# Output projections of two mixers as products of rounded halves, and modulation chunks moved, in a TensorE-bound float32 model on one core

## The reference

```python
def first_block(x, c, ...):
    for l in range(DEPTH):                      # DEPTH = 2; m = 3 l, 3 l + 1, 3 l + 2
        mod = (silu(c) @ ada_w[l] + ada_b[l]).reshape(b_, N_SUB, 3, D_MODEL)
        y = swiglu(modulate(x, mod[:, 0, 0], mod[:, 0, 1]), ffn_w13[l, 0], ffn_w2[l, 0])
        x = layer_norm(ALPHA * x + 0.5 * (1 + mod[:, 0, 2]) * y, ln_g[l, 0], ln_b[l, 0])
        y = token_mixer(modulate(x, mod[:, 1, 0], mod[:, 1, 1]), w_in[l], w_out[l], ...)
        x = layer_norm(ALPHA * x + (1 + mod[:, 1, 2]) * y, ln_g[l, 1], ln_b[l, 1])
        y = swiglu(modulate(x, mod[:, 2, 0], mod[:, 2, 1]), ffn_w13[l, 1], ffn_w2[l, 1])
        x = layer_norm(ALPHA * x + 0.5 * (1 + mod[:, 2, 2]) * y, ln_g[l, 2], ln_b[l, 2])

def token_mixer(h, w_in, w_out, ...):
    qkv_a, a_a, b_a, z_a, qkv_b, qk_c, v_c, i_c, f_c, o_c = jnp.split(h @ w_in, IN_SPLITS, axis=-1)
    ...   # oa: gated delta rule (384 wide), ob: attention (256), hc: mLSTM (384), each with its norm
    return jnp.concatenate([oa, ob, hc], axis=-1) @ w_out
```

## Time and profile before

| | before |
|---|---|
| median of 3 runs | 1808.94 us (1808.0 to 1812.43) |
| profiled execution | 1810.99 us, span 1809.2 us |
| mean granted TensorE clock | 0.986 of full speed |
| TensorE busy | 1714.5 us (95%), 12816 matmul records |
| VectorE busy | 1286.6 us (71%), 1938 instructions |
| ScalarE busy | 743.7 us (41%), 971 instructions |
| loads of ring chunks | 302 of 1024 KB, 5.6 us from issue to landing (median), and 2 of the condition |
| HBM read | 326.77 MB, 181 GB/s over the span |

### The profile page before, as it was taken

One profiled execution on the slowest core, in us unless ns is written; L12 is line 12 of the kernel. 1 busy time (PEld: TensorE's weight loads), 2 busy tenths in 40 slices (PEclk: granted clock), 3 DMA queues, 4 the chain that ended last, 5 costly groups with the idle time before them and its releaser, 6 DMA issues. The chain is left out here.

```text
span 1809.2 us, 30057 instructions
## 1 busy us (share of the span) xinstructions
PE 1714.5 (95%) x12816; PEld 1496.0 (83%) x12816; DVE 1286.6 (71%) x1938; ACT 743.7 (41%) x971; POOL 6.3 (0%) x14
## 2 busy tenths in 40 slices
PE   2999989999999999998899999999989999999998
PEld 2999979877999989998888789998834556747898
DVE  7876787856877786677976568897794778326744
ACT  2433375333533453335642264343322445224354
POOL 0000000000000000000000000000000000000000
PEclk9999999999999999999999999999989999999999
DMA  9877535443577737662546147774373010321102
GB/s 390 347 279 280 195 117 222 166 161 117 233 279 293 289 141 279 248 264 94 205 155 240 68 169 278 281 277 183 149 280 129 1 47 1 126 95 47 47 24 93
DMA packets 48516, 329.77 MB, mean 182 GB/s; under 512 B 5224, under 2 KB 8448, under 8 KB 9344
## 3 DMA queue, kind: packets, MB, share of 16 engines
q1 hardware_dynamic: 47520, 324.69, 46.7%
q0 software_dynamic: 864, 3.17, 0.6%
HBM read 326.77 MB, written 1.07 MB: 181 GB/s over the span
## 5 line engine op out<-in xcount | busy, mean ns | idle before, releaser
L332 PE MATMUL ps<-xhi,low 128*128 128x256 f32 x2048 | 501.1, 284 | 4.2 <-ACT xhi L1390 4.2
L332 PEld LDWEIGHTS ps<-xhi,low 128*128 128x128 f32 x2048 | 362.4, 192 | 5.9 <-ACT xhi L1390 5.2
L332 PE MATMUL ps<-xhi,whi_wk 128*128 128x256 f32 x1072 | 297.8, 287 | 39.8 <-ACT xhi L1390 38.9
L1390 ACT ACTIVATE wk<-ps 128x256 f32<-128x256 f32 (+5 forms) x219 | 108.6, 504 | 490.5 <-PE ps L332 425.0
L332 PE MATMUL ps<-xa,ring 128*128 128x256 f32 (+1 forms) x1056 | 287.0, 430 | 10.0 <-issue 4.8
L332 PE MATMUL ps<-xlo,whi_wk 128*128 128x256 f32 x1072 | 290.6, 280 | 0.0
L332 PEld LDWEIGHTS ps<-xa,ring 128*128 128x128 f32 x1056 | 200.4, 192 | 91.1 <-issue 62.0
L1390 ACT ACTIVATE whi_wk<-ring 128x2048 fp32r<-128x2048 f32 x100 | 191.5, 1918 | 159.2 <-DMA ring<-in_stream_dram 95.3
L332 PEld LDWEIGHTS ps<-xhi,whi_wk 128*128 128x128 f32 x1072 | 202.6, 194 | 42.8 <-issue 41.1
L1967 DVE TENSOR_TENSOR low<-ring,whi_wk 128x2048 fp32r<-128x2048 f32 (+1 forms) x101 | 228.4, 2264 | 6.6 <-ACT whi_wk L1390 6.6
L332 PE MATMUL ps<-wk 64*64 64x64 f32 (+10 forms) x2712 | 210.3, 262 | 5.8 <-ACT wk L1390 4.3
(11 more groups left out here) (131 smaller groups left out, 2547.9 us busy)
## 6 DMA issues: line engine op xcount, KB each, us to landing
ring<-in_stream_dram SPq DMA_DIRECT2D x302, 1024.0 KB, 5.6
ring<-in_cond_dram SPq DMA_DIRECT2D x2, 1024.0 KB, 4.8
wk<-spread_dram POOLq DMA_DIRECT2D x4, 384.0 KB, 5.2
wk<-spread_dram POOLq DMA_DIRECT2D x2, 768.0 KB, 7.5
tab<-in_tab_dram SPq DMA_DIRECT2D x1, 1440.0 KB, 20.4
res<-in_xt_dram SPq DMA_DIRECT2D x1, 1024.0 KB, 17.5
res<-in_ct_dram SPq DMA_DIRECT2D x1, 1024.0 KB, 9.2
out_dram<-wk SPq DMA_DIRECT2D x4, 256.0 KB, 2.4
```

The costliest lines, as they stand in the source:

```text
L332: last[0] = nc.tensor.matmul(o, l, r, start=start, stop=stop, skip_group_check=free)
L1390: return nc.scalar.activation(o, i, f, **kw)
```

## The change

- **Halves in the output projections** (m = 1 and 4). Each w_out chunk takes two places (`take_both`), so the four fill all eight. ScalarE rounds the four chunks (`out_weights_high`) and the eight result tiles (`result_high`, into `ohi`), VectorE makes both low parts (`out_weights_low`, `result_low`, into `whi_xa`), and each of the 64 products becomes three (`terms`). In TensorE's order "lx2" now stands ahead of `early(1, ...)`.
- **The mixer's start**: the `l2` sums move behind projection 5 and "p6.0"; ScalarE and VectorE copy projection 5 ahead of them (`gate_or_copy(9)`). The first chunk's halves are made in the FFN before (tile 20), and ScalarE's `normed` moves from the norm into the mixer, behind `win_high(m, 4)`. The rows r_u, r_ab and r_ln get other storage. `win_low(6)` goes ahead of `rows()`, and the wait for projections 3 to 5 moves to a later point on TensorE.
- **The norm behind a mixer**: the low parts of the next FFN's first two weight chunks move from the norm's start to behind the folded squares and behind the tokens' low parts.
- **Modulation chunks of m = 7**: six (FFN_MODS) go into FFN m = 3, two stay in MLA's front, which thus holds 6 instead of 16 chunks, and four (LAST_MODS) go into MLA's output projection. The condition is loaded four times instead of twice.

```diff
+        ohi = nc.alloc_sbuf_tensor_at("ohi", [P, KT, T], F32R, offset=wk_at + 4 * (SCR + 8960))
...
-        LATE_MODS = [(6, ch) for ch in range(GATE, 12)] + [(7, ch) for ch in range(12)]
-        LATE_AT = (0, 2, 4, 7, 10, 13, 16)
+        FFN_MODS = [(7, ch) for ch in range(6)]
+        LATE_MODS = [(6, ch) for ch in range(GATE, 12)] + [(7, 6), (7, 7)]
+        LATE_AT = (0, 1, 2, 3, 4, 5, 6)
+        LAST_MODS = [(7, ch) for ch in range(GATE, 12)]
+        COND_AFTER = (("var", 2), ("var", 4), ("var", 5), ("pt", MLA_H - 1))
...
+            return 0 if (m, ch) in FFN_MODS else 2 if (m, ch) in LATE_MODS else 3 if (m, ch) in LAST_MODS else 1
...
+                    if m == 3 and 2 <= p < 8:
+                        leave("ada", *FFN_MODS[p - 2])
...
-                    if i == 4:
-                        for p in range(3):
-                            eng.wait_ge(*step_of("proj_read", m, p))
-                        eng.wait_ge(scalar_done, step("l2sq", m))
-                        for t in range(6):
-                            mm(banks(1, 1536)[:, 256 * t:256 * t + 256], blk, tiles(g_sq, 256)[:, t], True, True)
-                        last[0].then_inc(tensor_done, 1)
-                        done.named("l2", m)
-                fill(2)
+                fill(1)
...
+                for p in range(3):
+                    eng.wait_ge(*step_of("proj_read", m, p))
+                eng.wait_ge(scalar_done, step("l2sq", m))
+                for t in range(6):
+                    mm(banks(1, 1536)[:, 256 * t:256 * t + 256], blk, tiles(g_sq, 256)[:, t], True, True)
+                last[0].then_inc(tensor_done, 1)
+                done.named("l2", m)
+                fill(1)
...
                 eng.wait_ge(vector_done, step("rows", m))
-                for p in range(3, 6):
-                    eng.wait_ge(*step_of("proj_read", m, p))
...
                 eng.wait_ge(scalar_done, step("ekd", m))
+                for p in range(3, 6):
+                    eng.wait_ge(*step_of("proj_read", m, p))
...
-                        w_out[ch] = tiles(take("wout", l, ch), 256)
-                        w_held[ch] = held[0]
-                    for k in range(5):
-                        mm(bank(ch, 256 * t, 256 * t + 256), w_out[ch][:, k, P * t:P * t + P], xa[:, k, CS], k == 0 and t == 0, False, free=True)
+                        no = w_held[ch] = take_both("wout", l, ch)
+                        w_out[ch] = tiles(low[:, (no + 1) % RING, :], 256), tiles(low[:, no % RING, :], 256)
+                        eng.wait_ge(vector_done, step("owlow", m, ch))
+                    terms(ch, t, (3, 4, 0, 1, 2))
+                def terms(ch, t, ks):
+                    (hi, lo), at_t, o = w_out[ch], slice(P * t, P * t + P), bank(ch, 256 * t, 256 * t + 256)
+                    for k in ks:
+                        if ch in (0, 1):
+                            eng.wait_ge(vector_done, step("ol", m, k))
+                        mm(o, hi[:, k, at_t], ohi[:, k, :], k == 3 and t == 0, False, free=True)
+                        mm(o, lo[:, k, at_t], ohi[:, k, :], False, False, free=True)
+                        mm(o, hi[:, k, at_t], whi_xa[:, k, XS], False, k == KT - 1, free=True)
                 eng.wait_ge(vector_done, step("oa_done", m))
                 eng.wait_ge(scalar_done, step("mo", m, 1))
+                fill(1)
                 early(1, 0)
                 early(1, 1)
...
-                fill(1)
...
-                        for k in range(5, 8):
-                            mm(bank(ch, 256 * t, 256 * t + 256), w_out[ch][:, k, P * t:P * t + P], xa[:, k, CS], False, k == KT - 1, free=True)
+                        terms(ch, t, (5, 6, 7))
...
+                leave("cond2", 3)
+                for c in range(4):
+                    leave("ada", *LAST_MODS[c])
...
+            def out_weights_high(m, ch):
+                n = found["chunk_no", "wout", m // 3, ch][1]
+                eng.wait_ge(landed[n % RING], loads(n))
+                eng.wait_ge(*step_of("chunk", n + 1 - RING))
+                act(low[:, (n + 1) % RING, :], ring[:, n % RING, :], ACT.Copy, "owround", m, ch).then_inc(scalar_done, 1)
...
+                if to_ffn:
+                    normed(m)
+            def normed(m):
...
+                    if kind == "w13" and j == 20 and f == 0:
+                        win_high(m + 1, 0)
+                    if m in (3, 5) and kind == "w13" and j == 2:
+                        conditions(m // 5)
...
                 win_high(m, 4)
+                normed(m - 1)
...
+                eng.wait_ge(tensor_done, step("proj", m, 5))
+                gate_or_copy(9, bank(6, 256, 512), "proj_read_a", m, 5)
                 one_table()
                 eng.wait_ge(tensor_done, step("l2", m))
                 log_mean(g_tt, banks(1, 1536), 1, EPS, "l2e", m)
                 root(g_tt, "ri", m)
...
                 fill(11)
+                out_weights_high(m, 1)
...
+                eng.wait_ge(tensor_done, step("oa", m))
+                for k in (3, 4):
+                    result_high(k)
+                eng.wait_ge(vector_done, step("oa_done", m))
+                for k in range(3):
+                    result_high(k)
+                for ch in (2, 3):
+                    out_weights_high(m, ch)
                 eng.wait_ge(vector_done, step("lcen", m))
                 act(l_sq, l_h, ACT.Square, "lsq", m).then_inc(scalar_done, 1)
+                out_weights_high(m, 0)
                 eng.wait_ge(tensor_done, step("lvar", m))
...
-                eng.wait_ge(vector_done, step("oa_done", m))
+                for k in range(5, 8):
+                    eng.wait_ge(vector_done, step("mix", m, k))
+                    result_high(k)
...
-                if to_ffn:
+                if to_ffn and m % 3 != 1:
                     lows(m + 1, 0)
-                elif m < 5:
-                    win_low(m + 1, 0)
+                elif m % 3 == 0:
                     win_low(m + 1, 1)
...
                 if m == 5:
                     context(0)
+                if m % 3 == 1:
+                    lows(m + 1, 0)
...
+                    else:
+                        lows(m + 1, 1)
...
+                        if m == 3 and 2 <= j // 2 < 8:
+                            mod_part(*FFN_MODS[j // 2 - 2])
...
+                def out_weights_low(ch):
+                    n = found["chunk_no", "wout", l, ch][1]
+                    eng.wait_ge(scalar_done, step("owround", m, ch))
+                    tt(low[:, n % RING, :], ring[:, n % RING, :], low[:, (n + 1) % RING, :].bitcast(F32), SUB, "owlow", m, ch).then_inc(vector_done, 1)
+                def result_low(k):
+                    eng.wait_ge(scalar_done, step("oh", m, k))
+                    tt(whi_xa[:, k, XS], xa[:, k, CS], ohi[:, k, :].bitcast(F32), SUB, "ol", m, k).then_inc(vector_done, 1)
+                out_weights_low(1)
                 fill(len(BESIDE) - at["n"])
+                for k in (3, 4, 0, 1, 2):
+                    result_low(k)
+                out_weights_low(2)
                 eng.wait_ge(tensor_done, step("lmu", m))
                 eng.wait_ge(vector_done, done.count)
                 stt(l_h, banks(6, 768), -1.0 / HD, l_h, MUL, ADD, "lcen", m).then_inc(vector_done, 1)
+                for ch in (3, 0):
+                    out_weights_low(ch)
                 eng.wait_ge(scalar_done, step("mixed_a", m))
...
+                for k in range(5, 8):
+                    result_low(k)
+                found["mixed", m] = found["ol", m, 7]
...
-                for c in range(6):
+                for c in range(2):
...
-                for c in range(6, 10):
+                for c in range(2, 4):
...
-                for c in range(10, 16):
+                for c in range(4, 6):
...
+                    if ch:
+                        mod_part(*LAST_MODS[ch - 1])
+                mod_part(*LAST_MODS[3])
```

More of the change, by code:

```diff
@@ L226, in build @@
         g_t, g_tt, g_dt, g_at, g_att = [W(SCR + 1536 * i, 1536) for i in range(5)]
-        r_u, r_ab, r_ln = [g_at[:, 256 * i:256 * i + 256] for i in range(3)]
+        r_u, r_ab, r_ln = W(23040, 256), W(23296, 256), r_rw
         g_sq = g_t
@@ L318, in scratch, with cond_of @@
         def scratch(m, ch):
-            return W(12800, D) if (m, ch) in LATE_MODS else W(6144, D)
+            return W(12800, D) if (m, ch) in LATE_MODS + LAST_MODS else W(6144, D)
+        def cond_of(m, ch):
+            return 0 if (m, ch) in FFN_MODS else 2 if (m, ch) in LATE_MODS else 3 if (m, ch) in LAST_MODS else 1
         block = ctx.enter_context(nc.Block())
@@ L447, in ffn @@
                         found["down", m, j] = found["down", m, j - 1] = found["chunk", held[0]]
-                    if m == 5 and p == 1:
-                        leave("cond2", 0)
+                    if m in (3, 5) and p == 1:
+                        leave("cond2", m // 5)
                     for ch in ada_of(m, p):
                         leave("ada", m + 1, ch)
```

(30 more changed lines are left out.)

10 lines of the change are left out of this document (4 added, 6 removed).

## The result

| | before | changed |
|---|---|---|
| median | 1810.68 us (4 runs, 1808.0 to 1813.31) | 1856.8 us (4 runs, 1849.64 to 1861.3) |
| ratio, 95% interval | | 1.0249 [1.0223, 1.0274] |
| profiled execution | 1810.99, span 1809.2, clock 0.986 | 1861.3, span 1859.5, clock 0.970 |

A forecast was written before the change was run, and what follows sets the result against it. TensorE, busy 95%, was taken to bound the kernel. The terms −2.2 + 2.4 + 23.2 + 8.4 + 0 − 12.6 + 6.2 = +25.4 on 1810.99 gave 1836.4; less 2.05, the forecast was 1834 us, range 1809 to 1846.

The forecast's parts named there:

- the wait at p7.0: Mixer's start: sign that TensorE would wait some 6 us at piece p7.0 for ScalarE's work behind the l2 sums.
- the three in the tail: Each mixer's tail: sign of three TensorE waits on VectorE of 5, 4 and 3.5 us, with a clock of 0.5.
- no gap at kr: MLA's front: sign that the 3.38 us gap, where ScalarE waits for kr made by VectorE behind six chunks, vanishes.
- (a): First norm of each layer: TensorE's 1.11 us wait for VectorE goes, −2.2 us for two layers.
- (b): Mixer start: the gap ahead of the l2 sums goes, a p7.0 wait with its clock comes; +2.4 us for both mixers.
- (c): Output projections: halves save TensorE 5.3 us a mixer, but three waits and 3.8 of clock make +23.2 for both.
- (d): Norm behind a mixer and next FFN's start: late loads, late squares and low parts, +4.2 us each, +8.4 together.
- (e): Six modulation chunks in the second layer's first FFN: covered by VectorE's idle third, 0 us.
- (f): MLA's front: ten of sixteen chunks leave, two gaps and their clock vanish, −12.6 us.
- (g): MLA's end: two chunks between the last residual and GLA's first tiles make TensorE wait, +6.2 us.
- R1: Rival in the mixers' tail: the halves are in time, −10.6 us in place of +23.2, total 1800; chance 0.15.
- R2: Rival in the mixers' tail: the waits come but the clock stays, 3.8 us less a mixer, total 1827; chance 0.2.

The follow-up runs named there:

- e3: The changed kernel with SP waiting, ahead of the load of the mixer's tenth input chunk, until GpSimd's three spread transfers have landed: 1838.56 us.
- e6: e3 with another order of VectorE's low parts in the mixers' tails, and TensorE multiplying chunk 1 ahead of lx2: 1812.47 us.
- e8: e1 with two ring places held per output chunk and the next FFN's low parts where the change has them: 1829.5 us.
- e2: The kernel before with only the moved modulation chunks and what serves them: 1804.34 us.
- e10: Kernel before plus first chunk's halves in the FFN, normalized tiles in the mixer, e3's SP wait, six modulation chunks in FFN m=3, ten in MLA's front: 1788.45 us.
- e12: e10 with the output projections as halves in the order of e6: 1797.53 us.
- e1: The changed kernel with fp32 output projections, one ring place per chunk, and the next FFN's low parts in their old places: 1817.39 us.
- e9: e3 with ScalarE's and VectorE's work at the mixers' start reordered (1846.54 us), and piece p7.1 also computed twice: 1845.96 us.
- e4: The changed kernel with the l2 sums, the copies of projection 5 and the low part of chunk 6 in their old places: 1849.91 us.
- e11: e10 with TensorE multiplying the table of ones by itself in the norms' waits, into a bank nobody reads: 1787.05 us.

## Why the prediction was wrong

Right way, wrong size: +50.3 in the profiled execution for +25.4. Every sign that the prediction named came: no gap ahead of the l2 sums, the wait at p7.0, the three in the tail, the late squares, no gap at kr, the longer wait at GLA. Most of the miss lies at a place for which it named none. By its parts:

- (a) −2.2: the norms give −1.3; 0.47 of the 1.11 us stayed.
- (b) **+2.4: measured +21.3. This is the step that failed.** The wait at p7.0 came as put, 6.3, and so did its clock: 48 records in 8.4 us where 5.6 is the rate. What the part left out is SP's queue: the change frees projection 5's places 10 us earlier (SP's next loads go out at 268.74, before at 279.16), and I did not ask which loads that lets go. The spread transfers stand in the sum at nothing, with no reason given. They met the spread transfers. The rows of that part are of ScalarE alone; none was of GpSimd's queue. e3 takes the collision away and 18 us with it. Most of it isn't the wait, 3.5 and 2.9 us, but the clock behind it: 6.3 and 6.2 us in the k k products and p13. Without these four terms +2.4 is left, the forecast. The prediction's price for a gap's clock, 2.5, came from rows where dense products follow.
- (c) +23.2: measured +24.5. The three waits came within 0.3 us, 12.6 together, and the clock took 3.7 a mixer for the 3.8 taken. The saving was sized wrong: 4.0 us a mixer, not 5.3, by e6's tail at the full clock, where 102 of the products take 12.39, 0.364 for three and not 0.353. 12.6 + 3.7 − 4.0 is the measured 12.2. e6 shows that the order made the waits.
- (d) +8.4: measured +13.5. The squares' +1.9 was +2.4, with 1.45 of clock in the twelve records behind it, which I had not counted; the low parts' +1.0 ahead of the tokens was 0; the FFN lost 3.0 and 2.8, a wait of 1.79 for the second low part at 486.16 (1.3 put) and the clock again. The norm's part is the full ring, as e8's trace shows; the FFN's wait is for the low part that stands late on VectorE.
- (e) 0: measured −0.4 with the norm's sums, and e2 agrees.
- (f) −12.6 and (g) +6.2: −13.1 in MLA's front and +6.3 at the wait ahead of GLA (9.47 for the 3.14 before), with −0.5 in GLA's products −7.3 for −6.4.

R1 asked whether the low part of the result starts before TensorE is ready. It didn't in the change; in e6's order it nearly does, and the tail then wins only 1.1 us, not 5.3, since 2.9 us of waits stay and the saving is 4.0. R2 took the clock out of the tail alone; with the 2.7 of part (b) it would have stood at 1821, not 1827. The range ended at 1846 because the upper bound of (b), +4.4 a mixer, held only a longer wait at p7.0; +10.7 was measured, with one more wait and its clock.

The rule of the Trainium skill named in the prediction ("TensorE: Matmul & The Clock Gate", "HAM oscillation — how this bites in real kernels") held in direction, and the rows at 0.50 agree; without the 3.7 us of clock the changed kernel's tail would have been 8.5 us longer a mixer, with it it was 12.2.

## What to carry to other kernels

- A removed wait also held something back. When TensorE releases buffers earlier, list the loads that start earlier and every transfer of other queues in those microseconds; e3 gave back 18 us with two waits ahead of a load that was wanted much later.
- Price a new wait by what runs behind it: ahead of dense products the lower clock cost 2.8 us, ahead of the small k k products 4.7 to 7.1, and shortening the wait from 4.4 to 1.7 us changed nothing in the kernel's time. Only its absence helped.
- Splitting a product into halves moves work to engines that may be in turn just then: order them first (e6, 26 us with the same work), and count the buffers that the halves hold. Here fp32 with a free ring won (e10 against e12, 9 us).

## What was not expected of the hardware

- Two 1 MB loads ahead of them made 6 KB stores take 3.5 us instead of 1.7. Two more, issued 0.6 and 1.0 us ahead of the 768 KB read, made it take 15.5 instead of 8.0; before, two loads issued 2.3 and 2.7 us behind it did not.
- The granted clock fell to 0.50 in the k k products behind a wait of only 1.4 us, though 48 (e1) and 72 (e9) dense products stood ahead of it, and stayed there until the p13 products were well under way. Without a wait the same products kept 1.00 in every profiled run. In e4 and e6, though, another chain of small products lost the clock without a wait (0.64 in e4's 386 to 394, 3.2 us); what decides it stays open. In e11 a few fp32 products in the norms' waits kept 1.00.
- A stretch at half the clock can cost little: four of them, gone in e11, gave 2.8 us of span, and the intervals of the two kernels overlap.
